# Convolution layer of a decoder trunk: eight phases instead of four, seven chunks on TensorE instead of six, and halved transposes in attention

## What is computed

```python
def conformer_conv_module(h, w_pw1, b_pw1, w_dw, b_dw, ln_g, ln_b, w_pw2, b_pw2):
    a = h @ w_pw1 + b_pw1
    u = a[..., :CONV_CH] * jax.nn.sigmoid(a[..., CONV_CH:])
    y = lax.conv_general_dilated(u, w_dw[:, None, :], window_strides=(1,),
        padding=[(CONV_WIDTH - 1, 0)], dimension_numbers=('NWC', 'WIO', 'NWC'),
        feature_group_count=CONV_CH) + b_dw          # width 31, one filter per channel
    y = jax.nn.silu(layer_norm(y, ln_g, ln_b))       # over the channels
    return y @ w_pw2 + b_pw2
```

## Time and profile before

| | |
|---|---|
| median of three executions | 1829.25 us |
| profiled execution | 1830.4 us, span 1828.5 us |
| TensorE busy | 99%, 1813.4 us |
| VectorE busy | 56% |
| ScalarE busy | 35% |
| mean granted clock of TensorE | 0.997 |
| DMA | 186 MB, mean 102 GB/s |

### The profile page before, as it was taken

How to read it: one execution, slowest core, us unless ns; L and a number is a source line. 1 busy time by engine, 2 the same in 40 slices (tenths; PEclk the granted TensorE clock), 3 DMA queues, 4 the chain that set the end, 5 groups by cost and what they waited for, 6 DMA issues and landing times.

```text
span 1828.5 us, 26076 instructions
## 1 busy us (share of the span) xinstructions
PE 1813.4 (99%) x9837; PEld 1512.8 (83%) x9837; DVE 1019.5 (56%) x1484; ACT 647.3 (35%) x977; POOL 31.1 (2%) x60
## 2 busy tenths in 40 slices
PE   9999999999999999999999999999998999999999
PEld 7888888887698888888888888888887988888887
DVE  6534434689767434434774344347898774344345
ACT  5322323455744213223442232224414542222223
POOL 1000000022000000000000000000000000000000
PEclk9999999999999999999999999999998999999999
DMA  6333332322032332333323223233454323333331
GB/s 199 117 99 103 92 100 91 122 84 80 4 102 92 97 99 92 103 92 97 111 92 102 93 92 103 92 102 105 175 167 138 93 94 102 92 92 104 92 103 58
DMA packets 64077, 186.08 MB, mean 102 GB/s; under 512 B 7264, under 2 KB 19168, under 8 KB 64000
## 3 DMA queue, kind: packets, MB, share of 16 engines
q1 hardware_dynamic: 61824, 182.69, 31.9%
q0 software_dynamic: 1600, 1.52, 0.3%
q10 hardware_dynamic: 576, 0.79, 0.1%
HBM read 179.08 MB, written 5.24 MB: 101 GB/s over the span
## 4 chain that ended last, share of the span: by engine, by line
PE 92%; DVE 5%; ACT 1%; issue 1%; DMA 0%; ACTq 0%; SPq 0%; DVEq 0%
PE bank L393 27%; PE bank L395 27%; PE bank L394 27%; PE bank L486 4%; DVE qT L1595 2%; PE bank L491 2%; PE bank L767 1%; DVE w_lo L1249 1%; PE bank L784 1%; PE bank L730 1%; PE bank L754 1%; PE bank L420 1%; PE bank L412 0%; PE bank L433 0%; DVE h_resid L1365 0%
## 5 line engine op out<-in xcount | busy, mean ns | idle before, releaser
L1249 DVE TENSOR_TENSOR w_lo<-w_raw,w_hi 128x1024 fp32r<-128x1024 f32 x302 | 369.3, 1225 | 419.3 <-ACT w_hi L962 408.6
L393 PE MATMUL bank<-x_hi,w_hi 128*128 128x512 f32 x1432 | 558.9, 390 | 0.0
L394 PE MATMUL bank<-x_lo,w_hi 128*128 128x512 f32 x1432 | 557.2, 389 | 0.0
L395 PE MATMUL bank<-x_hi,w_lo 128*128 128x512 f32 x1432 | 557.2, 389 | 0.0
L962 ACT ACTIVATE w_hi<-w_raw 128x1024 fp32r<-128x1024 f32 x302 | 317.1, 1055 | 561.9 <-PE bank L395 549.5
L393 PE MATMUL bank<-a_hi,w_hi 128*128 128x512 f32 (+1 forms) x894 | 331.5, 371 | 0.3 <-issue 0.3
L394 PE MATMUL bank<-a_lo,w_hi 128*128 128x512 f32 (+1 forms) x894 | 329.6, 369 | 0.0
L395 PE MATMUL bank<-a_hi,w_lo 128*128 128x512 f32 (+1 forms) x894 | 329.5, 369 | 0.0
L393 PEld LDWEIGHTS bank<-x_hi,w_hi 128*128 128x128 f32 x1432 | 268.8, 188 | 56.1 <-issue 0.7
L395 PEld LDWEIGHTS bank<-x_hi,w_lo 128*128 128x128 f32 x1432 | 268.8, 188 | 56.0
L394 PEld LDWEIGHTS bank<-x_lo,w_hi 128*128 128x128 f32 x1432 | 268.8, 188 | 55.5
(11 more groups left out here) (205 smaller groups left out, 1335.7 us busy)
## 6 DMA issues: line engine op xcount, KB each, us to landing
w_raw<-stream SPq DMA_DIRECT2D x312, 512.0 KB, 3.6
f_out<-mats_in SPq DMA_DIRECT2D x8, 576.0 KB, 6.3
tap_matrix<-mats_in SPq DMA_DIRECT2D x4, 576.0 KB, 7.7
h_resid<-xT SPq DMA_DIRECT2D x8, 256.0 KB, 5.7
qT<-stream SPq DMA_DIRECT2D x8, 256.0 KB, 5.9
u_scratch<-V SPq DMA_DIRECT2D x6, 256.0 KB, 2.4
a_lo<-u_scratch SPq DMA_DIRECT2D x6, 256.0 KB, 2.7
qT<-z_scratch SPq DMA_DIRECT2D x6, 256.0 KB, 4.2
```

Source lines behind the costliest of these rows:

```text
L393: nc.tensor.matmul(out, lw[0], lx[0], start=first, stop=False)
L394: nc.tensor.matmul(out, lw[0], lx[1], start=False, stop=False)
L395: return nc.tensor.matmul(out, lw[1], lx[0], start=False, stop=last)
L1249: nc.vector.tensor_tensor(w_lo[:, s, :], raw[:, s, :], w_hi[:, s, :].bitcast(F32), ALU.subtract).then_inc(s_lo, 1)
```

## The change

- `PH = 8`: eight phases of 64 places, 16 channels to a group of partitions, eight groups a chunk, five shifts instead of nine; a chunk is four pairs of groups, 80 matmuls of 64 columns. A tap matrix is 320 KB, and 13 have buffers (in `f`, in the unused part of `y`, in the spare tile and one new one).
- `NAT = 1`, `CONVS = 7`: one chunk stays on VectorE (31 taps), seven are on TensorE. Three of them (`EARLY = 3`) give the early mean. Each of the seven has a buffer for its groups.
- TensorE's order: chunks 0 to 2 each behind two slots, the early sum between slots 14 and 15, then the spread, chunks 3, 4, 5, four sums, chunk 6, four sums. Statistics lie on 64 partitions. Three of the 14 warm-up matmuls ahead of the deviation's broadcast and five of the eleven behind it go.
- The layer norm's output stays in phase order through silu and the second projection; the evacuation of the latter (`to_f`) puts it in token order.
- Attention: each transpose is done in two row halves of 64, into one PSUM bank each; the copy reads them together.

```diff
-PH = 4
+PH = 8
-NAT = 2
+NAT = 1
-EARLY = 4
+EARLY = 3
@@ build_program
-        conv_out = [two_banks[i] for i in (3, 2, 3, 2, 3, 0)]
+        conv_out = [two_banks[i] for i in (3, 3, 3, 3, 0, 1, 3)]
@@ sync
             def load_groups(i):
                 sp.wait_ge(s_ud[i % 2], 16 * (i // 2 + 1))
-                if i >= 2:
-                    sp.wait_ge(s_cv, PAIRS * (i - 1))
...
-                if j >= RING:
-                    load_matrices(j - RING + 1)
+                if j > RING:
+                    load_matrices(j - RING)
+                if j == KD - 1:
+                    for i in range(EARLY):
+                        store_z(i)
                 load(n + 1, (n + 1) % RING)
...
-            load_matrices(CONVS - 1)
-            for i in range(EARLY):
-                store_z(i)
+            load_matrices(KD - RING)
             sp.wait_ge(s_nat, NAT)
+            sp.wait_ge(s_cv, PAIRS * (EARLY + 2))
             for i in range(EARLY):
                 load_y(i)
+            store_z(3)
             store_z(4)
+            load_y(3)
+            store_z(5)
+            load_y(4)
+            load_y(5)
+            store_z(6)
             sp.wait_ge(s_sqmm, 1)
-            load_y(4)
-            store_z(5)
-            load_y(5)
+            load_y(CONVS - 1)
@@ tensor, attention
-                            last = nc.tensor.transpose(bank[6 + kb][:, j * P:(j + 1) * P],
-                                                       prob[t % 2][:, j, kb * P:(kb + 1) * P], ident[:, :])
+                            for rows in range(2):
+                                at, c = slice(rows * HALF, (rows + 1) * HALF), 4 * kb + j
+                                last = nc.tensor.transpose(bank[6 + rows][:, c * HALF:(c + 1) * HALF],
+                                                           prob[t % 2][at, j, kb * P:(kb + 1) * P], ident[at, at])
@@ tensor, convolution
                     for g in range(GROUPS):
-                        for part in range(2):
-                            to = slice(part * HALF, (part + 1) * HALF)
-                            ins = nc.tensor.matmul(out[to, 0:PH], src[:, g, to], same_q[:, 0:PH],
+                        ins = nc.tensor.matmul(out[0:NT, 0:PH], src[:, g, :], same_q[:, 0:PH],
...
                 first_body(n0, sub)
-                body(n0 + 6, 2)
+                for n in range(6, 8):
+                    body(n0 + n, n % RING)
                 for i in range(EARLY):
-                    for n in range(2 * i + 7, 2 * i + 9):
+                    for n in range(2 * i + 8, 2 * i + 10):
                         body(n0 + n, n % RING)
                     convolve(i)
+                body(n0 + 14, 2)
+                sum_early()
                 body(n0 + 15, 3)
-                sum_early()
-                convolve(4, range(0, 1))
                 pe.wait_ge(s_m0, 1)
                 spread_phases(BCAST, m0).then_inc(s_m0bc, 1)
-                convolve(4, range(1, 2))
-                convolve(5, range(0, 1))
+                for i in range(EARLY, CONVS - 1):
+                    convolve(i)
                 pe.wait_ge(s_nat, NAT)
...
+                sum_direct(BCAST, y[:, 0, :])
+                sum_centred(3)
+                sum_centred(4)
...
+                sum_direct(STAT, nat_sq[0])
+                convolve(CONVS - 1)
+                sum_centred(5)
+                pe.wait_ge(s_zsqadd, CONVS - 2)
+                sum_groups(STAT, zsq_sum, False, False)
+                sum_centred(6).then_inc(s_dlmm, 1)
+                pe.wait_ge(s_zsq, CONVS)
+                sum_groups(STAT, zsq[(CONVS - 1) % 2], False, True).then_inc(s_sqmm, 1)
@@ tensor, layer_norm
                 broadcast_phases(bank[6], dl).then_inc(s_lbc, 1)
-                keep_warm(3, out=5)
                 pe.wait_ge(s_linv, 1)
                 broadcast_phases(bank[7], std).then_inc(s_lbc, 1)
-                keep_warm(11, out=5)
+                keep_warm(6, out=5)
...
-                last_two(PW2, 4)
+                last_two(PW2, 4, at=lambda a, k, tok: by_phase(a[:, k, :])[:, :, tok.start // PH:tok.stop // PH])
@@ scalar, conv
-                    nc.scalar.activation(f[:, m, :].rearrange("p (n q) -> p q n", q=PH),
-                                         y[:, m, :].rearrange("p (q n) -> p q n", q=PH), ACT.Silu,
+                    nc.scalar.activation(f[:, m, :], y[:, m, :], ACT.Silu,
@@ vector, to_f
+                if how == "b_pw2":
+                    return nc.vector.tensor_scalar(by_token(f[:, m, tok]), by_phase(bank[b][:, tok]), col(how, m), None,
+                                                   ALU.add)
@@ vector, conv
+                        if e == 0 and 2 <= j < 6:
+                            k = taps(k, 4)
                         if (j, e) == (KD - 1, 0):
-                            k = taps(k, 6)
-                            biased(3)
...
+                            dve.wait_ge(s_m0mm, 1)
+                            nc.vector.tensor_scalar(m0[:, :], BCAST[:, 0:NT], 1.0 / (EARLY * P), None, ALU.mult
+                                                    ).then_inc(s_m0, 1)
+                            dve.wait_ge(s_m0, 1)
+                            for i in range(EARLY):
+                                centre(i)
+                            bias_less_mean(EARLY)
                     gate(j)
-                    if 2 <= j < KD - 1:
-                        k = taps(k, 3 if j == 2 else 4)
+                    if RING <= j < RING + EARLY:
+                        biased(j - RING)
+                        add_early(j - RING)
+                    if 2 <= j < 6:
+                        k = taps(k, 4 if j < 5 else 3)
...
+                direct_centred(0)
+                for i in range(EARLY + 1, CONVS):
+                    bias_less_mean(i)
+                    centred(i - 1)
```

More of the change, by code:

```diff
@@ L137, in build_program @@
                  for i in range(2)]
+        probT_halves = [fv[:, 2048 + i * 1024:2048 + (i + 1) * 1024].rearrange("p (b r q) -> p r b q", r=2, q=HALF)
+                        for i in range(2)]
         Vf = V[:, :, :].rearrange("p a n -> p (a n)")
@@ L232, in build_program @@
         s_ud = [sem(f"u_in_dram{i}") for i in range(2)]
-        s_ug = [sem(f"u_groups_loaded{i}") for i in range(2)]
+        s_ug = [sem(f"u_groups_loaded{i}") for i in range(CONVS)]
         s_zd = [sem(f"z_in_dram{i}") for i in range(4)]
@@ L380, in _ @@
             pool.wait_ge(s_mm, PW1)
-            for i in range(2):
+            for i in range(CONVS):
                 nc.gpsimd.memset(ug[:, i, :, 0:PAD], 0.0).then_inc(s_zeros, 1)
@@ L855, in sum_groups, with sum_centred @@
                     for g in range(GROUPS):
[L856 to L861 removed]
+                        ins = nc.tensor.matmul(out[0:NT, 0:PH], src[:, g, :], same_q[:, 0:PH],
+                                               start=(first and g == 0), stop=(last and g == GROUPS - 1),
+                                               skip_group_check=True)
+                    return ins
+                def sum_centred(j):
+                    pe.wait_ge(s_zc, j + 1)
+                    return sum_groups(BCAST, zg[j], False, j == CONVS - 1)
                 def sum_early():
[L864 removed]
+                    pe.wait_ge(s_rpre, sub + 1)
                     for j in range(EARLY):
@@ L869, in sum_early @@
                     last.then_inc(s_m0mm, 1)
-                def sum_rest(j):
-                    pe.wait_ge(s_zc, j + 1)
-                    sum_groups(BCAST, zg[j], False, j == CONVS - 1).then_inc(s_dlmm, 1)
-                def sum_direct(out, src, ready, first):
-                    pe.wait_ge(s_nsum, ready)
-                    for q in range(PH):
-                        for part in range(2):
-                            to = slice(part * HALF, (part + 1) * HALF)
-                            ins = nc.tensor.matmul(out[to, q:q + 1], src[:, q * NT + to.start:q * NT + to.stop],
-                                                   ones[:, 0:1], start=(first and q == 0), stop=False,
-                                                   skip_group_check=True)
-                    return ins
@@ L886, in sum_squares, with sum_direct @@
-                def sum_squares(added):
-                    if added:
-                        pe.wait_ge(s_root, 3 * sub + 1)
-                        sum_direct(STAT, nat_sq[0], 2, True)
-                        pe.wait_ge(s_zsqadd, CONVS - 2)
-                        sum_groups(STAT, zsq_sum, False, False)
-                        return
-                    pe.wait_ge(s_zsq, CONVS)
-                    sum_groups(STAT, zsq[(CONVS - 1) % 2], False, True).then_inc(s_sqmm, 1)
+                def sum_direct(out, src):
+                    for q in range(PH):
+                        nc.tensor.matmul(out[0:NT, q:q + 1], src[:, q * NT:(q + 1) * NT], ones[:, 0:1],
+                                         start=(q == 0), stop=False, skip_group_check=True)
@@ L926, in broadcast_phases @@
```

(27 more changed lines are left out.)

118 lines of the change are left out of this document (56 added, 62 removed).

## The result

The changed kernel takes 1834.19 us in the median (1830.66 to 1839.75) where the kernel before takes 1829.59 on the same chips: ratio 1.0025, 95% interval 1.0018 to 1.0032, 4.6 us slower. Its profiled execution took 1834.86, with a span of 1833.0; the span before was 1828.5. The forecast of 1822.2 is missed, and the time lies outside the range.

The account below looks back on a forecast made before the run. TensorE, busy for 99% of the span, was taken as the bound. Convolution -5.1, attention -2.2 and boundary +0.3 sum to -7.0 us, from the median of 1829.25 to 1822.2; range 1814.5 to 1831.

Parts of the forecast that it names:

- the attention's 2.2: Attention: transposes in row halves were to save 2.2 us in all, ends 0 and 4.5.
- the 4.4 that I had put to the clock: Convolution tail: lower clock adds 3.2 us on the broadcasts and, on average, 1.2 on the last chunk.
- 1.2 of clock: Second projection's start: lower clock adds 1.2 us on the warm-up and first matmuls.
- 0.3 of boundary: Boundary behind the second projection: two half evacuations with strided writes add 0 to 0.5 us, taken as 0.3.
- I take this 0.06 for a four of 64 columns: Convolution chunks: four quadrant matmul records take 0.06 us, bound by weight loads, so a chunk takes 2.8 us.
- Rival 2: Convolution: small matmuls don't keep a burst's rate, 0.029 us a record, a chunk 5.1; +6.1 us, 1835; chance 0.12.
- columns and loads explain every rate seen: Convolution: argument against a slower sustained rate of small matmuls, beside the burst of four starts after a pause.
- Rival 1: Convolution tail: clock holds or falls once briefly, at most 2 of 5.6 us lost; 1816 to 1820; chance 0.24.
- rival 3: Convolution tail: last chunk waits for groups or matrices, or both sum stretches lower the clock long; 1824 to 1829; chance 0.16.
- the bound: Attention's middle steps: VectorE, busy 26.4 of 28.3 us, is next, so at most 1.9 us in eight steps can go.
- a tile that is ready earlier brings nothing more: Second projection and boundary: TensorE is full behind 1406, so earlier tiles gain nothing.
- x1.7: Second projection: VectorE's evacuation with strided write takes 1.7 times as long, from 1.15 against 0.66 us.

Follow-up runs that it names:

- the quiet burst: Changed kernel plus 320 float32 matmuls of 64 columns with unused results at the end of attention, where DMA is nearly idle; 1852.21 us in one execution.
- chunk 3 was early: Changed kernel with chunk 3 convolved between the early sum and the last slot, not behind the spread; 1827.0 us, ratio 0.9984 to the kernel before.
- without z's traffic: Changed kernel with stores and loads of z cut to 8 of 128 partitions, TensorE's instructions the same; 1832.6 us in one execution.

## Why the prediction was wrong

Up to the last slot it was right. Its end was priced at 1369.3, with the attention's 2.2 at 1367.1; it was 1367.3. A chunk in the loop took 2.56 (2.8), VectorE kept up, the early sum waited for nothing. (One reading was off without weight: gates from 1337.28 to 1354.23 are a round of 16.95, not 16.97.) Only chunk 0 had a pause within it, and nothing in the forecast provided for that (TensorE's timeline, changed kernel):

```profile
1327.69 0.56 PE L864 MATMUL bank<-a_lo,qT 64*64 64x64 f32 x20 [0.84 <-issue]
```

Behind the last slot the terms came out so, in us:

| piece | priced at full clock | ran | pauses in it |
|---|---|---|---|
| spread | 1.9 | 1.73 | |
| chunks 3 to 5 | 7.6 | 9.15 | 6.37 |
| four sums | 4.1 | 5.20 | 2.06 |
| last chunk | 2.8 | 4.27 | |
| four sums | 4.1 | 4.37 | |
| two broadcasts | 3.7 | 7.02 | 0.34 |
| to the first matmul | 2.2 | 2.34 | |
| sum | 26.4 | 34.1 | 8.8 |

The span came out 11.5 us over the forecast (1833.0 for 1821.5). Of these 8.8 are the pauses, and 3.3 is what the work itself took beyond the 4.4 that I had put to the clock ahead of the projection's start: 34.1 - 26.4 = 7.7. A chunk and a sum at full clock took no more than was priced (2.56 for 2.8 and 1.02 for 1.03), so I put these 3.3 to the clock too. The last slot adds 0.2, and what lies behind the start takes 0.8 off: it grew by 0.75, where 1.2 of clock and 0.3 of boundary were priced.

**The step that failed** is "I take this 0.06 for a four of 64 columns" together with its use on chunks in a row. The rate itself is right: 128 records in 2.09. But it was read from bursts (8 and 32 records), and it was applied to 1280 instructions and 256 more of sums with no wide matmul between them. The two resources that I weighed, columns and weight loads, don't bind there; the third, which I didn't look for, is the supply of instructions: one block of 256 per 3.7 to 4.0 us in the quiet burst, and per 3.7 to 5.7 in the tail (1373.70, 1379.18, 1382.90 and 1388.56 are the starts behind its pauses).

**Rival 2** had the time (1835 for a measured 1834.2), and in the tail nearly its rate (0.029). That the time agrees is chance. Its mechanism, a rate that no small matmul exceeds, isn't the one: in the loop chunks run at 0.016 a record, and its last slot would have ended near 1376, where 1367.3 was measured. The rule of the Trainium skill that it came from ("TensorE: Matmul & The Clock Gate", section "Wait — 56ns, not 53.3ns?", no start to start below about 25 ns) doesn't hold for quadrants: 128 records in 2.09 us are 0.016. The point against it, that "columns and loads explain every rate seen", was true of the rates of before and yet no evidence: none of those rows holds more than 32 records below 128 columns.

**The clock** fell as forecast after the sums, and the broadcasts cost 3.3 more than at full level (3.2 priced). It fell once more than priced, in or behind pauses, so the pauses may have cost more than their 8.8; that isn't shown. On the other hand the lower clock hides the supply of instructions: chunk 6 took 0.027 a record (160 in 4.27), so 128 of them take 3.4 us, nearly a block's time, and no pause stands between 1388.56 and 1407.45. The two losses don't simply add. **Rival 1** is out: 23.8 us at the lower level. Of **rival 3** the first half is out for the changed kernel, in which no DMA released a wait of TensorE; its wait for matrices came up only once chunk 3 was early (1.6 us). Its second half, both stretches of sums at the lower clock for long, did come: 6.8 and 13.6 us, which is a part of the 3.3. Storing a gate's chunk took longer (5.3 for 2.4 us in the page's median), and no wait of TensorE came of it.

**The attention** gained 2.7 at the start of the convolution layer (VectorE's up_tmp there at 1299.50 for 1302.22), where 2.2 was priced, but some 1.1 to 1.3 in the medians, hardly clear of noise. A middle window, as in the earlier trace rows:

```profile
456.40:484.70 28.30, 27.66 (x294) 16.39 (x296) 27.19 (x85) 27.45 (x96) 0.00 (x0) 1.00 0.01 2
```

TensorE isn't full any more (27.66 of 28.30), and VectorE (27.2) and ScalarE (27.5) are nearly so; the bound had named VectorE. My step "a tile that is ready earlier brings nothing more" was right for the end of the layer and should have been asked of its start, too: time gained ahead of a tail with waits of its own arrives only in part.

**The evacuation by phase** costs VectorE 1.19 us for 0.75 where it is whole and 0.70 for 0.48 where it is half, x1.6 and x1.5 where x1.7 was priced (groups of VectorE from 1400 to 1470, shapes apart). The boundary hardly moved, where 0.3 was priced: from the end of the second projection to the norm's broadcast it takes 5.59 us (1456.87 to 1462.46) for 5.55 (1452.04 to 1457.59).

## What to carry to other kernels

Count instructions, not only columns and loads: a burst's rate holds for the instructions that are already there, and a long stretch of small matmuls runs at the rate at which blocks of instructions come in (here 256 in 3.7 to 4.0 us, up to 5.8 in the tail; a float32 matmul is four of them). Put such stretches between wide matmuls, where the next block mostly arrives unseen: moving one chunk of 320 instructions was worth 7.5 us and made a loss of 4.6 into a gain of 2.9, though with the old transposes only 2.7. Where a block ends depends on every instruction ahead of it, so a change far away moves the pauses: 112 more pairs of load and matmul in the attention moved them by 112 records. In a trace look for "issue" pauses at equal counts of instructions.

## What was not expected of the hardware

- Instructions ran out: after 422 of them in a row, then after each 256, with DMA at 33 GB/s. In the layer's tail two such starts were 5.48 us apart (1373.70 and 1379.18), and without z's traffic 5.81 (1377.46 and 1383.27).
- Four quadrants take small float32 matmuls at 0.016 us a record as long as there are instructions, with 64 columns each; with 128 columns it is 0.030 (80 records in 2.42).
- TensorE's clock stayed at 1.2 GHz for 17 us of full occupation, ten idle matmuls of 512 columns among them. What would have raised it is open.
